# Attention of a 1024-token prompt over compressed, selected and windowed keys: from a loop over query heads to an unrolled order of score units and probability rounds

## What is computed

```python
def _nsa_core(qc, qr, gates, q_pos, k_cmp, v_cmp, c2s, ks_b, vs_b, kw, vw, kw_pos):
    s = jnp.einsum('btkgd,bckd->bkgtc', qcg, k_cmp) * scale          # 63 compressed keys
    p_cmp = _masked_probs(s, cmp_end[None, :] <= q_pos[:, None])
    o_cmp = jnp.einsum('bkgtc,bckd->btkgd', p_cmp, v_cmp)
    imp = jnp.einsum('bkgtc,cs->bkts', p_cmp, c2s)                   # importance of 16 blocks of 64 keys
    score = jnp.where(visible, imp + jnp.where(forced, FORCED_BONUS, 0.0), NEG)
    top_val, top_idx = lax.top_k(score, n_top)                       # 8 of the 16 blocks
    ...
    p_sel = _masked_probs(s, sel_valid)                              # softmax over the 8 blocks
    o_sel = jnp.einsum('bkgtm,bktmd->btkgd', p_sel, v_sel)
    p_win = _masked_probs(s, (rel >= 0) & (rel < WINDOW) & (kw_pos[None, :] >= 0))   # 512 keys back
    o_win = jnp.einsum('bkgtl,blkd->btkgd', p_win, vw)
    o = o_cmp * g[..., 0:1] + o_sel * g[..., 1:2] + o_win * g[..., 2:3]
```

## Time and profile before

| what | us |
|---|---|
| median of 3 runs | 3833.59 (3832.59 to 3834.82) |
| the profiled execution | 3827.84 |
| its span | 3826.0 |
| mean granted TensorE clock, share of 2.4 GHz | 0.904 |
| PE busy / PEld busy | 3136.7 (82%) / 2038.5 (53%) |
| DVE / ACT / POOL busy | 1184.1 (31%) / 737.9 (19%) / 273.9 (7%) |
| prompt attention, from its first DMA issue to the next stage's | 1058 to 1596 |
| second group's products L2915 | 8.86 |

### The profile page before, as it was taken

One profiled execution on the slowest core, in us unless ns is written; L12 is line 12 of the kernel. 1 busy time (PEld: TensorE's weight loads), 2 busy tenths in 40 slices (PEclk: granted clock), 3 DMA queues, 4 the chain that ended last, 5 costly groups with the idle time before them and its releaser, 6 DMA issues. The chain is left out here.

```text
span 3826.0 us, 40607 instructions
## 1 busy us (share of the span) xinstructions
PE 3136.7 (82%) x13898; PEld 2038.5 (53%) x13898; DVE 1184.1 (31%) x2468; ACT 737.9 (19%) x1251; POOL 273.9 (7%) x291
## 2 busy tenths in 40 slices
PE   7886877775678999784566799667979999996999
PEld 4554546665556677552343344543446666664665
DVE  2333655453345555301230112221123323230000
ACT  3332431111023343200120111111111222120000
POOL 1110002221010101000000000000000010000000
PEclk9898988887589999897788899889989999998999
DMA  3111010001210000274755211352221111112211
GB/s 116 56 56 50 27 32 12 11 11 41 69 25 25 25 13 13 74 227 133 221 154 206 89 66 55 121 176 91 88 60 33 40 37 33 33 33 46 80 53 38
DMA packets 286044, 265.13 MB, mean 69 GB/s; under 512 B 68002, under 2 KB 250148, under 8 KB 285412
## 3 DMA queue, kind: packets, MB, share of 16 engines
q1 hardware_dynamic: 247684, 224.82, 18.8%
q10 hardware_dynamic: 38240, 38.84, 3.3%
HBM read 219.75 MB, written 48.04 MB: 70 GB/s over the span
## 5 line engine op out<-in xcount | busy, mean ns | idle before, releaser
L3030 PE MATMUL up_acc<-hnT,up_w 128*128 128x364 f32 (+1 forms) x2112 | 646.9, 470 | 11.6 <-DMA up_w<-in_w_up 11.6
L3030 PEld LDWEIGHTS up_acc<-hnT,up_w 128*128 128x128 f32 x2112 | 402.7, 191 | 255.5 <-issue 14.6
L3131 PE MATMUL down_acc<-mlp_gT,down_w 128*128 128x364 f32 (+1 forms) x1056 | 324.6, 471 | 29.9 <-DMA down_res<-scr_h2T 29.9
L3131 PEld LDWEIGHTS down_acc<-mlp_gT,down_w 128*128 128x128 f32 x1056 | 201.9, 191 | 152.6 <-issue 32.6
L391 PE MATMUL chan_acc<-xnT,chan_w 128*128 128x364 f32 (+1 forms) x576 | 185.6, 485 | 44.2 <-DMA chan_w<-in_w_in 28.1
L324 PE MATMUL proj_p<-proj_w_nat,proj_xT 128*128 128x512 f32 (+1 forms) x432 | 177.7, 575 | 14.2 <-ACT proj_xT L219 14.2
L391 PEld LDWEIGHTS chan_acc<-xnT,chan_w 128*128 128x128 f32 x576 | 112.7, 197 | 117.0 <-issue 53.9
L3069 DVE TENSOR_SCALAR up_y<-up_xp,up_tap 128x1024 f32<-128x1024 f32 x44 | 35.8, 812 | 425.0 <-ACT up_xs L3041 425.0
L324 PEld LDWEIGHTS proj_p<-proj_w_nat,proj_xT 128*128 128x128 f32 x432 | 88.2, 207 | 102.4 <-issue 79.7
L2590 PE MATMUL xo_p_h<-w_xo,xo_aT 128*128 128x512 f32 x288 | 128.0, 603 | 12.9 <-DVE xo_h L2545 10.7
L2612 PE MATMUL mixo_p_q<-w_xq,mixo_nT 128*128 128x512 f32 x288 | 127.6, 602 | 5.8 <-DVEq L2567 5.8
(11 more groups left out here) (538 smaller groups left out, 4443.5 us busy)
## 6 DMA issues: line engine op xcount, KB each, us to landing
up_w<-in_w_up SPq DMA_DIRECT2D x44, 512.0 KB, 4.5
sc_pg<-in_cache_cmp ACTq DMA_DIRECT2D x128, 128.0 KB, 2.8
sc_pg<-in_cache_cmp SPq DMA_DIRECT2D x128, 128.0 KB, 2.7
sa_ring<-in_cache_sel SPq DMA_DIRECT2D x128, 128.0 KB, 2.8
sa_ring<-in_cache_sel ACTq DMA_DIRECT2D x128, 128.0 KB, 2.8
down_w<-in_w_down SPq DMA_DIRECT2D x8, 1408.0 KB, 6.4
xs_kn<-in_cache_mem SPq DMA_DIRECT2D x8, 1024.0 KB, 6.7
xs_v<-in_cache_mem SPq DMA_DIRECT2D x8, 1024.0 KB, 9.5
```

The lines of the kernel that those rows point to most:

```text
L3030: m = pe.matmul(acc[n][:, g, 0:b - a], w[:, s, n, k, :], hnT[:, k, a:b], start=(k == 0), stop=(k == KD - 1))
L3131: m = pe.matmul(acc[s][:, g, 0:b - a], w[:, s, f, :], gT[:, f, a:b], start=(f == 0), stop=(f == FT - 1))
```

## The change

`stage_nsa_prompt_attend` is written anew, and its loops are gone: one generator `order()` gives a single list of steps, and every engine's program walks that list and issues its part of each step.

- A **unit** is one branch of one query-head position `g` (0 to 3) for both key/value heads at once: 8 units in a block, 64 in all. Its scores are two matmuls with 64 rows of weights, the one on partitions 0 to 63 and the other on 64 to 127, into two banks of one of two score slots `S[0]`, `S[1]` (L1471). A unit takes only the keys that its block can see: 128(b+1) for the selected branch, 128 min(b+1, 5) for the window, in pieces of at most 512. DVE masks and takes the minimum of the negated scores (L1668), ACT exponentiates (`exps`), and POOL, new in this place, scales the probabilities in SBUF by gate over sum (`scale`: three small instructions and two of the unit's width, L1572).
- A **round** is one tile of 128 keys of one branch, for all 8 heads: 8 transposes into `T` (L1482, two banks), one copy of both banks (1024 columns) to `pT`, by ACT where the round's number is even and by DVE where it is odd (L1684), and two matmuls with 64 columns of values as the weights, 512 columns of `pT` streaming, into the lower and the upper half of the partitions of `O[b % 2]` (L1433). There are 66 rounds: 2, 4, 6, 8, 10, 11, 12 and 13 for blocks 0 to 7. All three branches add up in PSUM, so the six small DVE instructions of each head go; the block's output is copied once (ACT), turned back with 4 transposes and copied again (ACT).
- The list goes in **periods** i from -2 to 8, of 8 slots each. Period i holds the front steps of block i+2, the units of block i+1 and the rounds of block i.
- The importance, the choice and the mask are computed only for blocks 4 to 7; the blocks before them can see at most 8 blocks of 64 keys and take the constant mask `near`.
- In `stage_cross_sample` the sequences `b` become the innermost loop of L2915.

```diff
@@ stage_prompt_keys @@
-                dve.memset(kw[:, 0:WIN], 0.0)
-                dve.memset(vw[:, 0:4, :], 0.0)
@@ stage_nsa_prompt_attend @@
+        def unit(b, u):
+            branch, g = (WINB, u) if u < G else (SEL, u - G)
+            n = P * (window_blocks(b) if branch == WINB else b + 1)
+            return branch, g, P * (b + 1) - n, n, [(lo, min(512, n - lo)) for lo in range(0, n, 512)]
+        FRONT = {0: "turn_q", 1: "cmp_scores", 2: "cmp_exp", 3: "cmp_norm", 4: "importance", 5: "top", 6: "turn_p", 7: "mask"}
+            for i in range(-2, NQ + 1):
...
+                for u in range(8):
+                    if i >= 1 and u in (2, 3):
+                        yield ("take_o", "turn_o")[u - 2], i - 1, 0
+                    if i + 2 < NQ:
+                        yield FRONT[u], i + 2, 0
+                    if 0 <= i + 1 < NQ:
+                        yield "unit", i + 1, u
+                    if 0 <= i < NQ:
+                        n = len(rounds_of(i))
+                        for r in range(u * n // 8, (u + 1) * n // 8):
+                            yield "round", i, r
...
             def _(pe):
-                            for k in range(lo, hi):
-                                v, c = (vs[:, k, :], 128) if what == "s" else (vw[:, ds(b + k, 1), :].rearrange("p a n -> p (a n)"), 256)
-                                m = pe.matmul(po[:, c:c + P], pT[:, r % 2, (k - lo) * P:(k - lo + 1) * P], v,
-                                              start=(k == first), stop=(k == end - 1))
+                    pe.wait_ge(*kept(n))
+                    for kv in range(KVH):
+                        pe.matmul(O[b % 2][HALF[kv], :], v[:, HALF[kv]], pT[:, n % 2, kv, :], start=False,
+                                  stop=(n + 1 == FIRST_ROUND[b + 1]), skip_group_check=True).then_inc(pv_done[kv], 1)
...
+                            pe.wait_ge(read, before)
+                            for kv in range(KVH):
+                                pe.matmul(out[:, kv, 0:n], qT[HALF[kv], b % 2, 1, g * P:(g + 1) * P], keys[HALF[kv], at + lo:at + lo + n],
+                                          start=True, stop=True).then_inc(scored[kv], 1)
+                    elif what == "round":
+                        pe.wait_ge(scaled, 2 * (8 * b + (4 if branch == WINB else 8)))
+                        if n:
+                            pe.wait_ge(*kept(n - 1))
+                                t = pe.transpose(T[:, kv, g * P:(g + 1) * P], probs(b, branch, G * kv + g)[:, c:c + P], ident[:, :])
+                        t.then_inc(t_done, 1)
...
+                        if n:
+                            use(n - 1)
             def _(pool):
+                def scale(m):
+                    pool.wait_ge(exp_done, KVH * (m + 1))
+                    pool.tensor_scalar(c, sums[:, b % 2, branch, g, :], 1e-30, None, ALU.max)
+                    pool.drain()
+                    pool.tensor_tensor(c, c, minus_one[:, :], ALU.pow)
+                    pool.drain()
+                    pool.tensor_tensor(c, c, gates[:, b, col:col + 13:12], ALU.mult)
+                    pool.drain()
+                    for kv in range(KVH):
+                        p = probs(b, branch, G * kv + g)[:, 0:n]
+                        pool.tensor_scalar(p, p, c[:, kv:kv + 1], None, ALU.mult).then_inc(scaled, 1)
             def _(dve):
+                                t = dve.tensor_tensor_reduce(probs(b, branch, G * kv + g)[:, lo:lo + n], out[:, kv, 0:n], mask, 1.0, -NEG,
+                                                             ALU.add, ALU.min, low_to)
+                            t.then_inc(read, 1)
...
-                        dve.wait_ge(t_used[1], before + (3 if wide else 2))
+                        dve.tensor_copy(pT[:, 1, :, :], T[:, :, :]).then_inc(odd_ready, 1)
@@ stage_cross_sample @@
-                    for b in range(4):
-                        r = slice(32 * b, 32 * b + 32)
-                        for n in range(2):
-                            for c in range(2):
+                    for n in range(2):
+                        for c in range(2):
+                            for b in range(4):
+                                r = slice(32 * b, 32 * b + 32)
```

More of the change, by code:

```diff
@@ L1354, in run @@
-        def run(eng, pair):
-            with eng.Fori(0, 2) as i:
-                pair(i, False, False)
-            pair(2, True, False)
-            pair(3, True, True)
-        def heads(i, wide, last):
-            for p in range(2):
-                b = 2 * i + p
-                for h in range(8):
-                    nxt = None
-                    if h < 7:
-                        nxt = (b, p, h + 1, 8 * b + h + 1)
-                    elif not (last and p == 1):
-                        nxt = (b + 1, 1 - p, 0, 8 * b + 8)
-                    yield b, p, h, 8 * b + h, nxt, not (last and p == 1)
+        scaled = st.sem("scaled")
@@ new lines, in stage_nsa_prompt_attend @@
+        ORDER = list(order())
+        FIRST_ROUND = [sum(len(rounds_of(c)) for c in range(b)) for b in range(NQ + 1)]
+        ROUNDS = [(b, branch, k) for b in range(NQ) for branch, k in rounds_of(b)]
+        slot_uses, piece_no, pieces = {}, {}, 0
+        for what, b, u in ORDER:
+            if what in ("turn_q", "cmp_scores", "turn_p", "turn_o"):
+                slot_uses[what, b] = len(slot_uses)
+            elif what == "unit":
+                for j in range(len(unit(b, u)[4])):
+                    slot_uses[what, b, u, j] = len(slot_uses)
+                    piece_no[b, u, j] = pieces = pieces + 1
@@ L1373, in stage_nsa_prompt_attend, with slot, kept, taken @@
+        def slot(*use):
+            n = slot_uses[use]
+            return S[n % 2], slot_read[n % 2], n // 2
+        def kept(n):
+            return (odd_ready if n % 2 else even_ready), n // 2 + 1
+        def taken(*use):
+            _, read, before = slot(*use)
+            return read, before + 1
+        def probs(b, branch, h):
+            return (p_win if branch == WINB else p_sel)[:, b % 2, h]
         with nc.Block() as block:
@@ L1499, in _, with use @@
-                for step in range(8):
-                    front(0, 0, step)
-                scores(0, 0, 0, True)
-                run(pe, pair)
+                def use(n):
+                    b, branch, k = ROUNDS[n]
+                    v = (vw if branch == WINB else vs)[:, k, :]
+                    pe.wait_ge(*kept(n))
+                    for kv in range(KVH):
+                        pe.matmul(O[b % 2][HALF[kv], :], v[:, HALF[kv]], pT[:, n % 2, kv, :], start=False,
+                                  stop=(n + 1 == FIRST_ROUND[b + 1]), skip_group_check=True).then_inc(pv_done[kv], 1)
@@ L1528, in pair @@
-                def pair(i, wide, last):
-                    for b, p, h, n, nxt, fronts in heads(i, wide, last):
-                        before = turns_before(n, wide)
-                        for r in (0, 2) if wide else (0,):
-                            act.wait_ge(t_done[0], before + r // 2 + 1)
-                            act.wait_ge(t_used[0], before + r // 2 + 1)
-                            act.activation(pT[:, 0, :], pt[0][:, :], ACT.Copy).then_inc(t_ready[0], 1)
-                            if r == 0 and fronts and h == 5:
-                                front(b + 1, 1 - p, h)
-                        if nxt:
-                            exps(*nxt, wide)
-                        if fronts and h != 5:
-                            front(b + 1, 1 - p, h)
@@ L1542, in _, with exps @@
-                act.sem_inc(turned_read, 1)
-                for step in range(8):
-                    front(0, 0, step)
-                exps(0, 0, 0, 0, True)
-                run(act, pair)
+                def exps(m):
+                    b, u = m // 8, m % 8
+                    branch, g, _, n, _ = unit(b, u)
+                    act.wait_ge(low_ready, m + 1)
+                    for kv in range(KVH):
+                        p = probs(b, branch, G * kv + g)[:, 0:n]
+                        act.activation(p, p, ACT.Exp, bias=low[:, b % 2, branch, g, kv:kv + 1], scale=-1.0,
+                                       accum_out=sums[:, b % 2, branch, g, kv:kv + 1]).then_inc(exp_done, 1)
```

546 lines of the change are left out of this document (262 added, 284 removed).

## The result

| | before | after |
|---|---|---|
| median of 4 runs, us | 3833.09 (3827.11 to 3834.82) | 3678.44 (3666.85 to 3681.33) |
| profiled execution / its span | 3827.84 / 3826.0 | 3666.85 / 3665.1 |
| prompt attention, first DMA issue to the next stage's | 537.0 | 394.2 |
| second group's products, cross attention | 8.86 | 3.64 |
| mean granted TensorE clock | 0.904 | 0.892 |

The ratio is 0.9594 (95% interval 0.957 to 0.9617). Faster, as forecast, but 63 us slower than the 3615 predicted, and 6 us beyond the upper end of the range. Of the 161.0 us between the profiled executions, 142.8 come from the prompt attention (328 us were predicted, 394.2 measured) and 10.4 from the cross attention.

What follows compares the result with a forecast made beforehand. PE was taken as the bound of the prompt attention. Longest engines by period, 242 us, plus start, clock, form, hand-over, softmax and end terms gave 328; 3827.84 - 210 - 9 = 3609, 3615 against the median, range 3565 to 3672.

Steps and rivals of the forecast that it cites:

- fifth rival: Prompt attention: POOL's scaling at some ns a column sets the end; at 6.25 ns stage 618, kernel 3905 us; chance 0.03.
- second rival: Prompt attention: POOL scales at the two-tensor rate, 1.86 ns a column; stage 355 us, kernel 3642; chance 0.13.
- lower clock: Prompt attention, periods -1 to 1: PE at the lower clock level has its work doubled, adding about 10 us.
- softmax: Prompt attention: the compressed scores' softmax stands ahead of masks on DVE, some 3.5 us in each of 6 periods, 20 us.
- form changes: Prompt attention, periods 4 to 7: some 116 changes of PE's weight form at 0.15 us each, 17 us.
- slots with two rounds: Prompt attention, periods 4 to 6: in 9 slots an odd first round's copy stands behind four masks on DVE, 11 us.
- The start: Prompt attention: queries loaded first, one block's front chain comes to some 21.5 us, 15.5 over the 6 already counted.
- rivals 1 and 6: Prompt attention: score pairs don't overlap, about 3645, chance 0.10; products aren't paired either, stage 398 us, time 3685, chance 0.03.
- Rival 3: Prompt attention: the hand-overs hide better, stage 295 to 300 us, time 3582; chance 0.12.
- PE waits mainly for POOL in periods 4 to 6: Prompt attention: a sign named beforehand that would show the forecast wrong; no size given.
- A granted clock below 0.9: Prompt attention, periods 4 to 6: a sign named beforehand that would show the forecast wrong.
- Rival 4: Prompt attention: the hand-overs cost more, 1 us more for each of 56 slots, time 3670; chance 0.10.

Runs made afterwards that it cites:

- e9: The changed kernel with POOL's two wide products taking the constant 0.5 instead of a column of factors; stage 383.7 us, median 3663.09 us, ratio 0.9557.
- e3: The changed kernel with POOL's wide scaling written as a product of two tensors, the factor repeated; stage 338.0 us, median 3615.43 us, ratio 0.9431.
- e2: The changed kernel with POOL's wide scaling replaced by a copy in place, probabilities left unscaled; stage 311.1 us, median 3585.95 us, ratio 0.9354.
- e1: The changed kernel with POOL's two wide scaling instructions cut to their first column; stage 307.2 us, median 3584.03 us, ratio 0.9351.
- e7: The changed kernel with head 0's wide scaling on DVE and head 1's on ACT; stage 318.7 us, median 3601.09 us, ratio 0.9412.

## Why the prediction was wrong, step by step

**What failed is one price.** "Only one wide operand is read, so I take the copy", 0.87 ns a column over 0.15 us. Measured: 2.5 over 0.29. With 67584 columns and 128 instructions that is 110 + 18 us more, as POOL's busy time says (125 more than with the copy). The dearest price from which I drew a case near the range, 1.86 ns, was too low as well: I had argued from the number of wide operands, and left aside the 2.6 ns a column of L952 in the earlier trace rows. A constant factor (e9) and a two-tensor product (e3) show that the kind of instruction sets the price, not the number of wide inputs. What the Trainium skill ("GPSIMD Engine Reference", 4.1 Engine selection) says, and I had set beside the choice, that one-input work on GpSimd runs at about line rate, holds for the copy, 1041 ns, and not for TENSOR_SCALAR, 2849 ns.

**What then set the stage** is the mechanism of the fifth rival, at a price between the second's and its own: POOL works from 1078.4 to 1422.6, 344 us, almost without a wait, with 23.6 us ahead of it and 26.4 behind. The ends are what the second rival's sum had for them (6 + 24 + 15.5 + 5 = 50.5). With the measured price that sum gives POOL 102 + 37 + 169 + 23 = 331 us, the stage 382 and the kernel 3669; of the 13 us by which POOL's stretch is longer, 11 are short gaps ahead of the wide instructions (5.6 and 5.4 us with the releaser "issue" in POOL's waits), for which I had no term. With the 2.6 ns of L952 and the fixed part as I had it, it would have been 145 + 176 = 321 for POOL and 3658 for the kernel. The fifth rival asked only from which price on the stage is as long as before (5 ns); that POOL sets the end begins far below, and between 1.86 and 5 ns no case of mine stood.

**The rest of the sum was 17 us too high** (e2: 311 against 328).
- Periods -1 to 1: predicted 56.5, 10 for the lower clock and some 7 for the softmax, 73.5 us; e2's row of 1079.3 to 1138.8 has 59.5 for them. The clock is low there (0.76), but PE is idle for 11 us in the stretch: POOL waits for work for less than 5 us of it (its drains don't count as busy), so the doubled work of PE and the stalls lay beside POOL's time, and I had added them up.
- Periods 2 and 3: predicted 58 and 7, 65 us; from 1138.8 to the first copy of queries in period 4, at 1205.8, it is 67.0.
- Periods 4 to 6: predicted 97.6 for the engines, 13 of the form changes, 11 for the slots with two rounds, 7 for softmax, 129 us; from the first output copy in period 4 to that in period 7 (e2's row of 1211.0 to 1336.2) it is 125.2.
- The start: 21.5 predicted from first issue to period -1; 1057.9 to 1079.3 is 21.4. The end: 5 predicted, 5.1 in the changed kernel (last output copy 1443.96, end 1449.04).
- Period 7: I put 24 + 8 us and 4 of the form changes, 36; e1's cycle of 2.37 for 13 rounds is 31. That cycle is set by T and its copies, and the form changes lie within the wait for them. In e2, period 7 and the end take 37.9 us, from the first transposes at 1331.1 to 1369.0, where 41 were predicted.
- Two sums of the prediction were added up wrongly: with no pairs PE has 112 + 58 + 112 + 14 + 26 = 322 us, not 332, and at 1.86 ns POOL has 145 + 126 = 271, not 277. Neither is in the forecast.

**The other points.** Pairs run at once, for scores as for products, so rivals 1 and 6 fall. DVE: 512 columns in 685 to 688 ns, the copy 1.22 us; ACT: 1142 and 713 ns, copy 1.02: as priced; the sums came out lower, 183 and 158 against 193 and 183. The cross attention gave 10.4 for 9. Of the signs, "PE waits mainly for POOL in periods 4 to 6" came true only one step further: by name it waits 1.2 us for POOL there, and 12.5 behind DVE's waits for the importance sums. A granted clock below 0.9 did not: it was 0.92 in these periods (1.00 in e2). It was 0.79 in periods 2 and 3, where PE, kept waiting, was busy 66 of 104 us. Rival 2's price (1.86) is near e3's (1.63 over 0.23 us), which took 338 us where 355 were said. Rival 3 (the hand-overs hide better, stage 295 to 300) was nearer than the forecast for the rest of the sum: at the copy's price the stage is 311 us and the kernel 3586, for 3615 and the 3582 of the rival. Rival 4 (the hand-overs cost more) thus has no part in the miss.

What stays open: why GpSimd's TENSOR_SCALAR is dearer than its two-tensor product, and the 12 us by which e7's stage is longer than e1's, of which I know only that PE waits 7 us longer for DVE's copies (18.4 and 11.3).

## What to carry to other kernels

Where a change gives an engine an instruction that the trace doesn't hold, no neighbour bounds its price from above: ask from which price on that engine sets the end, and give the prices on the way there a case and a chance. Wide work that is moved to an idle engine is free only until it is the longest; here the same product cost 2849 ns on GpSimd, 1893 written another way, 750 on VectorE and 1138 on ScalarE. Of two terms that delay different engines in the same stretch, only the longer counts.

## What the runs showed of the hardware that I had not expected

- GpSimd, 1024 f32 columns: COPY 1041 ns, TENSOR_TENSOR with a repeated factor 1893, TENSOR_SCALAR 2849 with a column of factors and 2776 with a constant.
- An instruction of VectorE on two columns with two SBUF inputs took 0.80 us beside a two-tensor product of GpSimd, and ended with it (595 ns in the mean of 32); 157 ns with one input.
- Matmuls with 64 rows of weights on the two halves of the partitions run at once: four of them, two of 512 and two of 384 columns, in 1.70 us with the change of form.
- Four column strips 32 wide run four deep: 32 records of 512 columns in 3.64 us, where the order with neighbours in the same strip took 8.86.
